# Samples' query latents for two heads per product: block-diagonal queries, key weights turned in one piece

## What is computed

```python
def mla_sample(q_nope, q_rope, ckv_new, kr_new, cache_lat, cache_kr, page_table, w_uk, w_uv):
    ...
    q_lat = jnp.einsum('bshn,rhn->bshr', q_nope, w_uk)    # b: 8 samples, h: 8 heads, n: 64, r: 128
    s_past = jnp.einsum('bshr,btr->bhst', q_lat, lat_past) + jnp.einsum('bshp,btp->bhst', q_rope, kr_past)
    s_new = jnp.einsum('bshr,btr->bhst', q_lat, ckv_new) + jnp.einsum('bshp,btp->bhst', q_rope, kr_new)
    ...
    p = jax.nn.softmax(s, axis=-1).astype(lat_all.dtype)
    o_lat = jnp.einsum('bhst,btr->bshr', p, lat_all)
    return jnp.einsum('bshr,rhv->bshv', o_lat, w_uv)
```

## Time and profile before

| | us |
|---|---|
| median of 3 executions | 750.83 |
| lowest, highest | 748.47, 752.94 |
| the profiled execution | 752.8 |
| its span, first to last instruction | 751.0 |
| TensorE busy (95% of the span) | 713.6 |
| VectorE busy (47%) | 356.1 |
| ScalarE busy (44%) | 327.1 |
| GpSimd busy (10%) | 75.5 |
| mean granted clock of TensorE, share of 2.4 GHz | 0.982 |

### The profile page before, as it was taken

The page is one execution under the profiler, slowest core; times in us unless marked ns, Lnnn a source line. Parts: engine busy times, 40 slices in busy tenths (PEclk is TensorE's granted clock), DMA queues, the critical chain, the costliest instruction groups (busy, mean ns, idle before and its releaser), DMA issues.

```text
span 751.0 us, 16689 instructions
## 1 busy us (share of the span) xinstructions
PE 713.6 (95%) x7025; PEld 551.8 (73%) x7025; DVE 356.1 (47%) x782; ACT 327.1 (44%) x779; POOL 75.5 (10%) x113
## 2 busy tenths in 40 slices
PE   2799999999999989999989999999999999999995
PEld 1487878788789977777755577776668999668884
DVE  0454370030202125878655756675662121379977
ACT  1254651211212146677544644665757667602100
POOL 0000000000000011000121122011212443000000
PEclk9999999999999999999979989999999999999999
DMA  9996300303001020000010200020654885103332
GB/s 296 396 350 181 112 1 1 113 0 95 1 12 45 9 69 17 9 15 9 10 12 1 56 1 2 1 58 1 199 209 178 286 285 206 59 1 115 112 140 84
DMA packets 35301, 70.31 MB, mean 94 GB/s; under 512 B 6626, under 2 KB 17979, under 8 KB 33564
## 3 DMA queue, kind: packets, MB, share of 16 engines
q1 hardware_dynamic: 30602, 47.73, 19.5%
q0 software_dynamic: 4016, 20.97, 8.1%
q10 hardware_dynamic: 610, 0.55, 0.3%
HBM read 62.26 MB, written 6.07 MB: 91 GB/s over the span
## 4 chain that ended last, share of the span: by engine, by line
PE 92%; DVE 3%; ACT 2%; issue 1%; DMA 1%; ACTq 1%; POOL 0%; DVEq 0%; POOLq 0%
PE banks L1978 21%; PE banks L2164 8%; PE banks L1990 6%; PE banks L2293 5%; PE banks L2374 4%; PE banks L2394 4%; PE banks L2142 3%; PE banks L2522 2%; PE banks L2524 2%; PE banks L2523 2%; PE banks L2080 2%; PE banks L1999 2%; PE banks L2462 2%; PE banks L2481 2%; PE banks L2505 2%; PE banks L2506 1%
## 5 line engine op out<-in xcount | busy, mean ns | idle before, releaser
L1022 ACT ACTIVATE s_z<-banks 128x512 f32<-128x512 f32 (+3 forms) x40 | 19.6, 501 | 130.0 <-PE banks L1978 130.0
L1978 PE MATMUL banks<-s_w_parts,s_h_b 128*128 128x272 f32 (+3 forms) x328 | 68.1, 323 | 0.0
L1231 ACT ACTIVATE s_z<-banks 128x512 f32<-128x512 f32 (+1 forms) x88 | 41.5, 517 | 54.2 <-PE banks L2374 54.1
L1405 DVE COPY s_zs<-banks 8x512 f32<-8x512 f32 (+3 forms) x6 | 3.5, 576 | 118.5 <-PE banks L1952 118.5
L1978 PEld LDWEIGHTS banks<-s_w_parts,s_h_b 128*128 128x128 f32 x328 | 49.3, 189 | 4.9 <-issue 1.7
L1978 PE MATMUL banks<-s_w_parts,s_h_a 128*128 128x256 f32 (+2 forms) x256 | 49.7, 314 | 0.0
L1222 ACT ACTIVATE s_z<-banks,s_temps 128x128 f32<-128x128 f32 (+7 forms) x64 | 47.1, 741 | 5.1 <-DVE s_temps L1705 4.7
L1978 PE MATMUL banks<-s_z_r,s_h_b 128*128 128x512 f32 (+1 forms) x152 | 48.8, 387 | 0.0
L2374 PEld LDWEIGHTS banks<-s_ident,s_z 128*128 128x128 f32 x288 | 34.4, 144 | 11.7 <-issue 6.0
L2164 PE MATMUL banks<-s_kt,s_temps 96*128 96x512 f32 (+1 forms) x96 | 42.2, 565 | 0.0
L2374 PE MATMUL banks<-s_ident,s_z 128*128 128x128 f32 x288 | 41.2, 280 | 0.1
(11 more groups left out here) (388 smaller groups left out, 1507.5 us busy)
## 6 DMA issues: line engine op xcount, KB each, us to landing
s_z<-in_w_ada SPq DMA_DIRECT2D x16, 512.0 KB, 12.1
s_temps<-in_w_in SPq DMA_DIRECT2D x3, 2048.0 KB, 7.7
s_x<-in_x_prompt SPq DMA_DIRECT2D x8, 512.0 KB, 11.9
s_z<-in_w_ada SPq DMA_DIRECT2D x1, 4096.0 KB, 14.1
s_kt<-in_w_out SPq DMA_DIRECT2D x8, 512.0 KB, 5.1
s_temps<-in_x_prompt SPq DMA_DIRECT2D x8, 512.0 KB
out_y_prompt<-s_temps SPq DMA_DIRECT2D x7, 512.0 KB
s_temps<-in_w_in SPq DMA_DIRECT2D x2, 832.0 KB, 14.0
```

What stands on the lines that cost most here:

```text
L1231: nc.scalar.activation(PTb[r % 3][:, 4 * g:4 * g + n, :], banks[:, 4 + (groups(r) + g) % 2, 0:P * n].rearrange("p (j q) -> p j q", j=n), A ...
L1978: last = nc.tensor.matmul(banks[:, proj_bank(c, t), 0:WIDTH[c]], h_[half][:, k, n0:n0 + P], w_, start=(k == 0 and n == 0), stop=(k == KT - ...
```

## The change

The latents of two heads come from one product. The queries of a pair of heads lie block-diagonally: rows 0 to 63 hold the even head's queries in the first 8 columns, rows 64 to 127 the odd head's in the other 8, and the rest is zero, set once by GpSimd. Against them stand the key weights of both heads, turned together: four transposes of 128x128 in one piece `wT` in place of eight of 128x64 in two. To bring the odd head's queries to rows 64 to 127, the unrotated queries are turned by plain matmuls with the identity instead of transposes. `PREP` loses one name, and `SLOTS` its last entry.

```diff
-            "T1", "q0", "q1", "gate", "wT0", "wT1", "qT", "qlat", "init", "T2",
+            "T1", "q0", "q1", "gate", "wT", "qT", "qlat", "init", "T2",
...
-        SLOTS = [(i, v) for i in range(PAIRED) for v in (1, 2, 3) if (i, v) >= (0, 3)] + [(i, h) for i in range(PAIRED, T) for h in (1, 4)]
+        SLOTS = [(i, v) for i in range(PAIRED) for v in (1, 2, 3) if (i, v) >= (0, 3)] + [(i, h) for i in range(PAIRED, T) for h in (1, 4)][:-1]
...
-                    for v in (s_cqT, qlw, qrw):
+                    for v in (s_cqT, qlw, qrw, s_ql):
                         nc.gpsimd.memset(v, 0.0).then_inc(p_padded, 1)
...
-                if n in (PREP["wT0"], PREP["wT1"]):
-                    q = n - PREP["wT0"]
+                if n == PREP["wT"]:
                     act.wait_ge(p_pe, n)
-                    nc.scalar.activation(w_ukT[:, 4 * q:4 * q + 4, :], banks[0:NOPE, 7, :].rearrange("p (h r) -> p h r", h=4), ACT.Copy).then_inc(p_free, 1)
+                    nc.scalar.activation(w_ukT, banks[:, 7, :].rearrange("p (m r) -> p m r", m=H // 2), ACT.Copy).then_inc(p_free, 1)
...
-                if n == PREP["wT1"]:
+                if n == PREP["qT"]:
                     dve.wait_ge(p_ln, 1)
                     nc.vector.scalar_tensor_tensor(out=s_la, in0=s_zn, scalar=-1.0 / TAU, in1=s_zm, op0=ALU.mult, op1=ALU.add).then_inc(p_la, 1)
-                if n == PREP["qT"]:
                     dve.wait_ge(p_pe, n)
-                    dve.wait_ge(p_padded, 4)
-                    nc.vector.tensor_copy(s_ql, banks[0:NOPE, 7, 0:64].rearrange("p (h b) -> p h b", h=H))
+                    dve.wait_ge(p_padded, 5)
+                    for par in range(2):
+                        rows = slice(NOPE * par, NOPE * par + NOPE)
+                        nc.vector.tensor_copy(s_ql[rows, :, par, :], banks[rows, 7, 0:H // 2 * NB].rearrange("p (m b) -> p m b", m=H // 2))
...
-                if n in (PREP["wT0"], PREP["wT1"]):
-                    for h in range(4):
-                        c0 = NOPE * (4 * (n - PREP["wT0"]) + h)
-                        last = nc.tensor.transpose(banks[0:NOPE, 7, P * h:P * h + P], w_uk[:, c0:c0 + NOPE], ident[:])
+                if n == PREP["wT"]:
+                    for m in range(H // 2):
+                        last = nc.tensor.transpose(banks[:, 7, P * m:P * m + P], w_uk[:, P * m:P * m + P], ident[:])
                 if n == PREP["qT"]:
                     pe.wait_ge(p_q4, 4)
                     for h in range(H):
-                        nc.tensor.transpose(banks[0:NOPE, 7, NB * h:NB * h + NB], sq[:, QK * h:QK * h + NOPE], i8)
+                        rows, c0 = slice(NOPE * (h % 2), NOPE * (h % 2) + NOPE), NB * (h // 2)
+                        nc.tensor.matmul(banks[rows, 7, c0:c0 + NB], sq[:, QK * h:QK * h + NOPE], i8, start=True, stop=True)
...
                 if n == PREP["qlat"]:
-                    for h in range(H):
-                        last = nc.tensor.matmul(banks[:, 7, NB * h:NB * h + NB], w_ukT[:, h, :], s_ql[:, h, :], start=True, stop=True)
+                    for m in range(H // 2):
+                        last = nc.tensor.matmul(banks[:, 7, 2 * NB * m:2 * NB * m + 2 * NB], w_ukT[:, m, :], s_ql[:, m, :, :].rearrange("p a b -> p (a b)"),
+                                                start=True, stop=True)
```

More of the change, by code:

```diff
@@ L293, in hybrid_step @@
         s_cqT = carve(2 * 32, 2, 32)
-        s_ql = carve(H * NB, H, NB, rows=NOPE)
+        s_ql = carve(H * NB, H // 2, 2, NB)
         s_decT = carve(2 * NB, 2, NB)
@@ L320, in hybrid_step @@
         s_ss = sb("s_ss", [NB, 8])
-        w_ukT = carve(H * P, H, P, rows=NOPE)
+        w_ukT = carve(H // 2 * P, H // 2, P)
         assert taken[0] <= MLA_AT
@@ L1194, in samples_piece @@
                     nc.scalar.activation(s_o, banks[0:NB, 7, :].rearrange("p (t c) -> p t c", t=2), ACT.Copy).then_inc(p_free, 1)
-                if n == PREP["wT0"]:
+                if n == PREP["wT"]:
                     act.wait_ge(p_zn, 1)
@@ L1660, in samples_piece @@
                     nc.vector.tensor_copy(s_decT, banks[:, 7, 0:16].rearrange("p (k b) -> p k b", k=2)).then_inc(p_free, 1)
-                    dve.wait_ge(p_padded, 5)
+                    dve.wait_ge(p_padded, 6)
                     for hp in range(2):
@@ L1763, in _ @@
             largest(0)
-            dve.wait_ge(p_padded, 7)
+            dve.wait_ge(p_padded, 8)
             for n in range(NSTEPS):
```

## The result

The changed kernel took 756.49 us (median of 8 executions, 754.45 to 759.45), the kernel before in the same series 749.88 us (746.73 to 758.99). The ratio is 1.0078, with a 95% interval of 1.0045 to 1.0112. It is slower: the whole interval lies above 1, though its lower end is a little under the half percent that the prediction took as the least that can be told. The forecast was 752.8. The time lies 0.01 us inside the upper end of the range, and the outcome, slower, is the one to which the prediction gave 0.26.

A forecast was written before the change was run, and what follows sets the result against it. TensorE bounds the kernel, 92 percent of the chain. From a median of 750.8 us: work -1.0 and waits +1.3 and +1.7 (together +2.0), old clock fall -1.5, new fall +1.5, giving 752.8; range 748.8 to 756.5.

The forecast's parts named there:

- The work: TensorE's own work: key turning -0.38, latents -0.94, query passes +0.29, together -1.0 us (-1.4 to -0.4).
- The waits: TensorE idle 1.7 us before the samples' query passes, 1.3 before later query transposes, 1.7 before the keys' third group.
- in every other place I find the cover holds: Claim that beyond the waits worked out, no moved piece makes TensorE wait for its producers.
- The old fall: Clock at 0.50 from 437.2 to 444.0 us, behind the latents; expected to go, worth 3.0 us of at most 3.4.
- The credit by half: For the median, only 1.5 us credited for the fall at 437, since not every execution seemed to have both falls whole.
- I take +1.5 (0 to 3.4): Cost in us of a new clock fall expected in step (2,2), near 420 us, partly hidden by the 1.3 us wait.
- the wait of 1.36: TensorE waiting for VectorE ahead of the query transposes of (2,3); forecast 1.3 us in place of 0.89.
- the wait of 1.84: TensorE idle ahead of the samples' query passes in (2,2), waiting for VectorE's rotated-query copies; forecast 1.7 us.
- the wait of 1.78: TensorE idle in (4,4) ahead of the keys' third group, waiting for GpSimd's product; forecast 1.7 us (1.4 to 1.9).
- a rival of its own: A second clock fall behind the 1.7 us wait at the keys' third group: +1.7, 754.5, with the long fall 756.4; chance 0.10.
- The fall at 386: Clock at 0.50 from about 386 to 396.2 us in the kernel before; the forecast gave it no change.
- The long fall: Rival: the new clock fall at (2,2) lasts 6.8 us, nothing hidden, costing 3.4: 754.7 us; chance 0.24.

The follow-up runs named there:

- slots_kept: Changed kernel with the pieces in the slots they had before the change, so the new arithmetic alone: 748.70 us, ratio 0.9966 to the kernel before.
- q4_early: Changed kernel with VectorE rotating the samples' queries one piece earlier, at (1,3) instead of (2,1): 753.47 us, ratio 1.0022 to the kernel before.
- both_early: Changed kernel with q4_early's earlier rotation, and GpSimd making the third group's keys ahead of the rotation of tile 5's queries: 752.56 us, ratio 1.0023.
- small_gathers: Changed kernel with each gather from the sixth on fetching a quarter of its bytes: 757.15 us, ratio 1.0077 to the kernel before.
- slots_kept_again: Second run of slots_kept, the changed kernel with the pieces in their old slots: 749.08 us, ratio 0.9983 to the kernel before.
- slots_rotation: slots_kept with the rotation of the samples' queries moved to (1,3), as in q4_early: 747.36 us, ratio 0.9957 to the kernel before.
- all_three: both_early plus VectorE's copies of the samples' queries placed after mask, maximum and normalising of (2,2): 753.99 us, ratio 1.0039 to the kernel before.
- waits_added: Changed kernel with 18 waits on a long-set semaphore at TensorE's start, nine more instructions in the trace: 758.11 us, ratio 1.0091 to the kernel before.

## Why the prediction was right, and where it wasn't

**The work: right.** -1.1 us against -1.0, part by part: -0.41 (forecast -0.38), -0.97 (-0.94), +0.28 (+0.29). The arithmetic alone gives 1.1 ±0.4 in executions at one clock. The row of L2590, taken for the query passes, held: 35 ns. The Trainium skill, "TensorE: Matmul & The Clock Gate", section on LDWEIGHTS, would have these passes at 53 ns as an estimate from 64 columns. The trace has 35 (16 passes in 0.56 us), and the measurement decides.

**The waits: right in place and size, one missed.** Forecast 1.7, 1.3 and 1.7 us, measured 1.84, 1.36 and 1.78. The step "in every other place I find the cover holds" failed in (3,3): TensorE idles 0.65 us there for query copies on ScalarE, in every profile with moved slots. There TensorE's own piece had become shorter while VectorE's had not. That and the tenths of the others make +3.9 us of new waits in place of the +3.0 of the sum, and +2.8 us without the clock in place of +2.0.

**The old fall: right.** None of the 12 profiles with halved latents has a fall at 437, both profiles of the kernel before do. The credit by half, 1.5 us, was near too: the clock share of slots_kept is 2.0 us (±1.1), though other falls have a part in it. The reason for taking 3.0 and not 3.4 for the whole fall holds in part: the 32 one-column passes take 1.80 us at half clock in the kernel before (439.09 to 440.89) and 1.10 at full clock in the changed one (433.96 to 435.06), so the fall costs them 0.70 and not 0.90. The reason for halving is borne out as well. 52 of 117 executions of the kernel before have a mean clock of 0.990 or more, while its two profiles, with both falls, have 0.982 and 0.978.

**The new falls: right in kind, too small in the sum.** The step that failed is "I take +1.5 (0 to 3.4)" for what the moved pieces do to the clock. Against slots_kept the mean clock falls by 0.0063, which is 4.3 us ±1.3. Of this some 1.3 only fills the wait of 1.36, so about 3.0 us is lost. Three things in the profiles stand beside it:
- A fall came near 420 in five of the six profiles with the wait of 1.84 and without the earlier rotation. It was 3.4 us long in four of them, half the old one, as the forecast took it, and 6.8 in one. Of q4_early and both_early, which lack the wait of 1.84, neither has it. The short one only filled the wait of 1.36. The prediction had seen that this wait hides a part; it hides all of it, and the term for this one place was too large.
- A second one came behind the keys' passes in two of the six profiles that have the wait of 1.78 (the changed kernel's first, and small_gathers). The prediction gave this 0.10 as a rival of its own. It belongs into every forecast, with some chance.
- The fall at 386 stands ahead of everything that moved, and the prediction took it as given. It is there in all nine profiles with moved slots, 6.8 or 10.2 us long, and in one of the three of the new arithmetic in the old slots (slots_kept, 6.8, against slots_kept_again and slots_rotation). It would be the largest part: 8.7 us on average against 2.3, some 2.9 us of time by the line. But both profiles of the kernel before have it too, 10.2 us long, with the slots unmoved, so it isn't tied to moved slots. Nor can the executions decide it. 1 of 20 of the changed kernel reaches a mean clock of 0.990, and 20 of 24 of slots_kept do, so low time is rarer in slots_kept. Where it is missing the mean doesn't say: the profiled execution of slots_kept has 0.990, with the fall at 386. That the move lengthens this fall is not shown.

**The sum.** In means over all executions: work -1.1, waits +3.9, old fall -2.0, new falls +3.0, together +3.8, and measured is 755.77 - 752.04 = +3.7. The two clock terms are themselves worked out from the means and the line, so what this tests is the rows of work and waits: +2.8 beside +2.7 at one clock. The forecast had -1.0, +3.0, -1.5 and +1.5, together +2.0. The rest of the miss (752.8 against 756.5) lies in the median. The executions of the kernel before lean to the low side (median 751.4, mean 752.0), those of the changed kernel to the high side (756.2 and 755.8). So the medians lie 4.8 us apart where the means lie 3.7, and 6.6 apart in the first series of 8 executions each. The range held by luck, by 0.01 us: the forecast stood 3.7 us low, and the upper end had been set for a long fall and a second one, which neither profile of the changed kernel has together.

**The rivals.** The long fall, with which the 754.7 was worked out, didn't come near 420 except in small_gathers (6.8 us) and all_three (6.7). By the rule of the Trainium skill, "TensorE: Matmul & The Clock Gate", section "PE-mode transpose", that transposes don't count as busy in the same way, it would have been the usual one; four of the five falls there were 3.4 us long. What stands beside the slower side is a sum of small things: a missed wait, a second place for a fall, and more low time elsewhere, the fall at 386 perhaps. No single rival held it, and "754.5, with the long fall 756.4" had the right number for another reason.

**What stays open.** Whether the fall at 386 depends on the slots behind it, and how; what stops TensorE between 570 and 620 us, and at a fixed count of instructions before 360; where the rest of the 2.5 us of waits_added goes.

## What to carry to other kernels

A piece that is dropped from a hand-placed order moves all behind it by a slot, and each of them then meets producers that were placed for the old slot. Keep the slots and leave the hole: the arithmetic alone was 1.1 us of work and 3 us of mean time faster (1.3 and 2.6 by the two ratios), and with the hole closed 3.7 us slower (5.9 and 3.4). On a saturated TensorE a wait costs its own length and, with some chance, a fall of the clock behind it: taking away the wait of 1.8 us at the keys' passes gained 3.8 (±1.8), of which the wait is 1.9. Look at both sides of a moved piece: the wait in (3,3) came because TensorE's piece in (3,2) got shorter and VectorE's did not. Where single executions scatter by more than the effect, set each one's time against its own mean clock: two kernels of 12 to 20 executions each can then be told apart to some 0.7 us, with a fall that hides a wait corrected by hand.

## What the runs showed of the hardware

- **Time follows the mean granted clock within 1 us** over 255 executions from 744.6 to 763.3 us. Nearly all of the scatter of a kernel goes with how long its clock stands low.
- **A fall can be free.** At half clock for 3.5 us around 420, TensorE ended 0.06 us later, since the slower passes filled a wait of 1.36.
- **Where the clock falls differs between executions of one program.** The changed kernel fell at 385 and 466.8 once, and at 384.9 and 418.9 the next time.
- **TensorE stops with no semaphore at fixed places.** 0.4 to 0.9 us each, two or more times between 570 and 620 us, in every profile but the first of the kernel before, and at three or more places between 290 and 360 us in all 14. In the changed kernel's timeline:

```profile
577.74 0.60 PE L2402 MATMUL banks<-s_ident,s_w_uq 128*128 128x128 f32 x4 [0.67 <-issue]
...
594.78 0.31 PE L2466 MATMUL banks<-s_z,s_temps 128*32 128x128 f32 x2 [0.39 <-issue]
```

"Issue" is time in which the engine waited for nothing that the profile shows. Of the stops before 360 us, those from L2097 at 312 us on stand at rows 4546, 5057, 5570, 6081 and 6593 of TensorE's instructions in the trace (weight loads, matmuls and semaphore waits, counted from 0), 511 to 513 apart. With nine more instructions ahead of them they stay at these rows to within one, and so fall on other matmuls. The stops between 570 and 620 us kept to their matmuls instead, to within one or two, in waits_added, and stayed with a quarter of the gathers' bytes; in some profiles the first of them is two shorter ones, some ten matmuls earlier. slots_rotation, the fastest, has them too, at L2394 and L2465:

```profile
PE banks L2465 <- issue: 1.5, 3, 0.9
PE banks L2394 <- issue: 1.2, 2, 0.7
```
